# The last chunk of the input projection made by seven block products, with its weight sums and sigmoid around the SSM's group norms

## The reference

```
h = concat(meta_tokens, x)
u = rmsnorm(h, norm_mix_w)
proj = u @ w_in                     # hq hf hi hg | mq mk mv mo | z xbc | gates
y_a = hgrn2(...)      ; group_rmsnorm * silu(g)
y_b = mlstm(...)      ; group_rmsnorm(h, norm_w, 4 heads) * sigmoid(o_pre)
y_c = mamba2(...)     ; group_rmsnorm(y * silu(z), norm_w, 4 groups)
h = h + concat(y_a, y_b, y_c) @ w_out
h = h + moe(rmsnorm(h, norm_ffn_w)) # top group, top 2 experts of it, w1 w3 w2
out = rmsnorm(h, final_norm_w)[16:]
```

## Time and profile before

| | |
|---|---|
| time, median of 3 runs | 1479.79 us (1478.51 to 1480.06) |
| profiled execution, span | 1478.6 us |
| TensorE busy | 1273.7 us, 86% |
| weight loads of TensorE busy | 762.6 us, 52% |
| DVE / ACT / GpSimd busy | 536.3 / 280.4 / 211.7 us |
| moved by DMA | 487.76 MB, 330 GB/s in the mean |
| granted TensorE clock, mean | 0.916 of full |

### The profile page before, as it was taken

One profiled execution on the slowest core, in us unless ns is written; L12 is line 12 of the kernel. 1 busy time (PEld: TensorE's weight loads), 2 busy tenths in 40 slices (PEclk: granted clock), 3 DMA queues, 4 the chain that ended last, 5 costly groups with the idle time before them and its releaser, 6 DMA issues.

```text
span 1478.6 us, 20527 instructions
## 1 busy us (share of the span) xinstructions
PE 1273.7 (86%) x8658; PEld 762.6 (52%) x8658; DVE 536.3 (36%) x1204; ACT 280.4 (19%) x424; POOL 211.7 (14%) x158
## 2 busy tenths in 40 slices
PE   9999999999999999877876787688768867797797
PEld 7898899879999994222322232223223222232243
DVE  3554567434533215532332232223222321322235
ACT  3212414112150023111111111111111110110003
POOL 3180055015525720000000000000000000000000
PEclk9999999999999999988888888988888887798799
DMA  8653353445358649999999999999999999999997
GB/s 239 214 171 113 95 143 115 150 135 168 114 183 332 228 147 420 433 428 431 432 430 430 433 432 433 431 433 430 433 430 433 431 430 433 428 409 426 435 429 335
DMA packets 106769, 487.76 MB, mean 330 GB/s; under 512 B 19996, under 2 KB 91960, under 8 KB 92760
## 3 DMA queue, kind: packets, MB, share of 16 engines
q1 hardware_dynamic: 104176, 481.01, 80.8%
q0 software_dynamic: 1392, 5.47, 1.1%
q10 hardware_dynamic: 1130, 0.24, 0.1%
HBM read 482.36 MB, written 4.61 MB: 329 GB/s over the span
## 4 chain that ended last, share of the span: by engine, by line
PE 54%; DMA 43%; DVE 1%; issue 1%; POOL 1%; ACT 0%; SPq 0%; DVEq 0%; POOLq 0%
DMA big<-in_moe_w_dram 42%; PE bank L1748 22%; PE bank L2192 8%; PE bank L2107 5%; PE bank L2221 3%; PE bank L2234 3%; PE bank L1861 2%; PE bank L2161 2%; PE bank L2205 2%; PE bank L1898 1%; PE bank L1874 1%; DMA big<-in_w_in_dram 1%; PE bank L1940 1%; DMA big<-in_x_dram 1%; PE bank L2294 0%
## 5 line engine op out<-in xcount | busy, mean ns | idle before, releaser
L2192 PE MATMUL bank<-big 128*32 128x512 f32 x2016 | 295.0, 740 | 183.7 <-DMA big<-in_moe_w_dram 182.4
L1748 PE MATMUL bank<-big 128*128 128x128 f32 (+4 forms) x2288 | 361.2, 318 | 0.9 <-DVE colc L1170 0.5
L1748 PEld LDWEIGHTS bank<-big 128*128 128x128 f32 x2288 | 322.3, 191 | 30.6 <-issue 1.1
L2192 PEld LDWEIGHTS bank<-big 128*32 128x32 f32 x2016 | 74.6, 132 | 400.4 <-issue 211.1
L1581 DVE COPY big<-bank 128x512 f32<-128x512 f32 x32 | 22.1, 692 | 504.5 <-PE bank L2192 503.8
L1594 DVE TENSOR_TENSOR big<-big,bank 128x512 f32<-128x512 f32 x240 | 146.2, 681 | 12.3 <-PE bank L2234 12.3
L2221 PE MATMUL bank<-big 128*32 128x512 f32 x992 | 128.0, 662 | 0.5 <-DVE big L1586 0.5
L2234 PE MATMUL bank<-big 32*128 32x512 f32 x480 | 126.9, 633 | 0.7 <-ACT big L1029 0.7
L712 POOL COPY big<-big 32x512 f32<-32x512 f32 x4 | 2.4, 604 | 758.8 <-ACT big L1053 758.6
L1016 ACT ACTIVATE big<-bank 128x512 f32<-128x512 f32 x32 | 19.1, 597 | 355.1 <-PE bank L2161 355.1
L2221 PEld LDWEIGHTS bank<-big 128*32 128x32 f32 x992 | 31.8, 119 | 91.1 <-issue 90.1
(11 more groups left out here) (357 smaller groups left out, 1107.5 us busy)
## 6 DMA issues: line engine op xcount, KB each, us to landing
big<-in_moe_w_dram SPq DMA_DIRECT2D x92, 4096.0 KB, 32.6
big<-in_w_in_dram SPq DMA_DIRECT2D x25, 2048.0 KB, 8.3
big<-in_w_out_dram SPq DMA_DIRECT2D x7, 2048.0 KB, 8.2
big<-in_moe_w_dram SPq DMA_DIRECT2D x5, 2048.0 KB, 30.2
big<-in_moe_w_dram SPq DMA_DIRECT2D x6, 1024.0 KB, 6.9
h_rows<-big SPq DMA_DIRECT2D x1, 2176.0 KB, 13.8
big<-gate_rows POOLq DMA_DIRECT2D x8, 272.0 KB, 4.6
big<-h_rows SPq DMA_DIRECT2D x1, 2176.0 KB, 12.8
```

The lines of the kernel that those rows point to most:

```text
L1748: last = V.matmul(outs, a, b, start=start and j == 0, stop=stop and j == n - 1)
L2192: last = V.matmul(pb[2 + r][CAP * g:CAP * (g + 1), :], xsT[:, k % 4, k // 4, :], wk, start=j == 0, stop=j == 3)
```

## The change

`FOLD` gets chunk 25. With it:
- TensorE makes chunk 25 by seven block products, blocks 0 to 3 where its first half stood and 4 to 6 where the second half stood.
- GpSimd makes four more weight sums, behind the pair sum of the SSM's squares. They use the same places as before (in `xv`), so `rs4z` moves from `xv` to `mv`.
- ACT copies the first block product, and the sigmoid of the chunk is one instruction in place.
- The DVE makes the adds, three and two of them before the SSM's norm and two behind it.
- The first tiles of the output projection wait for those adds to have emptied their PSUM banks.
- Since `FOLD[-1]` is 25, SP reads `h` back behind chunk 27's load, and not behind chunk 26's.

```
--- before.py
+++ after.py
@@ -152,7 +152,7 @@
         PHs = PHb.rearrange("p (h c) -> p h c", h=4)
         mlo = PHb[:, 0:4 * T].rearrange("p (h t) -> p h t", h=4)
         mden = PHb[:, 4 * T:5 * T]
-        rs4z = xv[:, :, :].rearrange("p a c -> p (a c)")[:, 0:4 * T].rearrange("p (h t) -> p h t", h=4)
+        rs4z = mv[:, :, :].rearrange("p a c -> p (a c)")[:, 0:4 * T].rearrange("p (h t) -> p h t", h=4)
         Wb = scr(2 * 4 * T)
         W = [Wb[:, i * 4 * T:(i + 1) * 4 * T].rearrange("p (h t) -> p h t", h=4) for i in range(2)]
         sq8 = Wb.rearrange("p (h t) -> p h t", h=8)
@@ -225,7 +225,7 @@
         oh = part(13056, NA * CAP).rearrange("p (a s) -> p a s", a=NA)
         wo = part(13120, NA * P).rearrange("p (a c) -> p a c", a=NA)
         wT = part(13376, NA * P)
-        FOLD = (4, 5, 6, 11, 12, 13, 14, 19, 20, 21, 22, 23, 24)
+        FOLD = (4, 5, 6, 11, 12, 13, 14, 19, 20, 21, 22, 23, 24, 25)
         NF = len(FOLD)
         HT = T // 2
         START, cur = [], 0
@@ -667,10 +667,11 @@
             pool.wait_ge(s["e_ready"], SSH // 2)
             spread_rows(floor_rows, SSH + MLH, MLH).then_inc(s["floor_rows_in"], 16)
             for c in FOLD:
-                if 17 < c:
+                if 17 < c < 25:
                     weight_sums(c)
             pool.wait_ge(s["sq_ready"], 3)
             V.tensor_tensor(sq8[:, 0:4, NM:T], sq8[:, 0:4, NM:T], sq8[:, 4:8, NM:T], ALU.add).then_inc(s["pairs_added"], 1)
+            weight_sums(25)
 
 
             def fold1(c):
@@ -954,11 +955,12 @@
             squares(s["ssm_gated"], 1, proj[:, Z0:Z0 + 8, :].rearrange("p (g j) t -> p j g t", j=2),
                     sq8.rearrange("p (j g) t -> p j g t", j=2))
             inverse_rms(1, 1, rs4)
+            first_product(25)
             act.wait_ge(s["in_ev"], 4 + 50)
             V.activation(proj[:, MO:MO + 2, NM:T], proj[:, MO:MO + 2, NM:T], ACT.Sigmoid).then_inc(s["z_gate"], 1)
-            tile_out(50, ACT.Sigmoid)
             inverse_rms(2, 2, rs4z)
-            tile_out(51, ACT.Sigmoid)
+            act.wait_ge(s["in_ev"], 4 + 52)
+            V.activation(proj[:, MO + 2:MO + 4, NM:T], proj[:, MO + 2:MO + 4, NM:T], ACT.Sigmoid).then_inc(s["z_gate"], 1)
 
 
             def token_squares(a, rows, sums_to, junk):
@@ -1202,15 +1204,18 @@
                 dve.wait_ge(s["fold_added"], 4 * n + 2)
                 add(hi0, lo1, 3).then_inc(s["fold_added"], 1)
 
-            def adds_b(c):
+            def adds_b(c, parts=(0, 1)):
                 if c not in FOLD:
                     return
                 n = FOLD.index(c)
                 add, lo0, lo1, hi0, hi1 = block_adder(c)
-                dve.wait_ge(s["fold_ps"], 5 * n + 5)
-                dve.wait_ge(s["fold_added"], 4 * n + 3)
-                add(hi1, hi0, 4)
-                add(lo1, lo1, 4).then_inc(s["fold_added"], 1)
+                if 0 in parts:
+                    dve.wait_ge(s["fold_ps"], 5 * n + 5)
+                    dve.wait_ge(s["fold_added"], 4 * n + 3)
+                    add(hi1, hi0, 4)
+                    add(lo1, lo1, 4).then_inc(s["fold_added"], 1)
+                if 1 not in parts:
+                    return
                 dve.wait_ge(s["in_tile"], 2 * c + 1)
                 dve.wait_ge(s["in_ev"], 4 + 2 * c)
                 dve.wait_ge(s["fold_added"], 4 * n + 4)
@@ -1481,9 +1486,11 @@
             adds_a(24)
             adds_b(24)
             step.link(group_norm(1, mlo, rs4, 4, 1, PL))
+            adds_a(25)
+            adds_b(25, (0,))
             group_norm(2, proj[:, Z0:Z0 + 8, :], rs4z, 4, 2, PS).then_inc(s["z_done"], 1)
-            dve.wait_ge(s["z_gate"], 3)
-            dve.wait_ge(s["in_ev"], 4 + NIN)
+            adds_b(25, (1,))
+            dve.wait_ge(s["z_gate"], 4)
             for h in range(MLH):
                 last = V.tensor_tensor(proj[:, MO + h, :], proj[:, MO + h, :], mlo[:, h, :], ALU.mult)
             last.then_inc(s["norm_done"], 1)
@@ -2065,7 +2072,10 @@
                 c = u // 2
                 if u % 2 == 0:
                     pe.wait_ge((s["in_a"], s["in_b"])[c % 2], 16 * (c // 2 + 1) + (16 if u == NIN + NOUT - 2 else 0))
-                pe.wait_ge(s["in_ev"], u + 1)
+                if c - 1 in FOLD:
+                    pe.wait_ge(s["fold_added"], 4 * (NF - 1) + 3 + u % 2)
+                else:
+                    pe.wait_ge(s["in_ev"], u + 1)
 
             def by_rows(k):
                 pe.wait_ge(s["in_ev"], 4 + NIN + (k // 2 * 2 + 2 if k < NOUT - 2 else k + 1))
```

## The result

The changed kernel takes 1482.36 us (median of 11 runs, 1481.77 to 1482.73), the kernel before, on the same chip, 1478.58 (11 runs): ratio 1.0021, 95% interval 1.0013 to 1.0029. That is 3.8 us slower.

The account below looks back on a forecast made before the run. TensorE was taken to bound the kernel through the output projection, then expert-weight loads. Products -1.1 and chunk 28's lateness +2.3 gave +1.2 us on the median 1479.79: 1481.0 us, range for 8 in 10 1478.4 to 1483.6.

Parts of the forecast that it names:

- the likeliest case's own range: Whole kernel: the time range for the forecast case itself, 1480.0 to 1482.2 us; that case had chance 0.50.
- rival B: Output projection: slow queue, chunk 28 landing past 471.2, slower by more than 0.2%; price +4.0, 1483.8 us, chance 0.13.
- TensorE's own work: Chunk 25: folded products take 12.70 us instead of 13.81, gain 1.11 us, or 1.23 at the folded w_out rate.
- GpSimd, ACT, DVE at nothing: Around chunks 25 and 26: the added sums, copies, adds and shifted norms all come in time, cost nothing.
- The reload: SP's queue: h, now ahead of the first expert load and chunk 28, makes chunk 28 late, costing 2.3 us.
- the chunk is late by ... 2.3 us: Chunk 28: TensorE waits 1.7 us for its load and 0.6 us for GpSimd's third sum.
- The 0.6 for the third sum: Chunk 28: GpSimd's third sum, ending 7.2 us behind the landing, is wanted 6.6 us after TensorE's start.
- Bounds: Chunk 28's lateness: sum -0.4 at the best queue rate, -1.1 if all is hidden, +4.0 at the slow rate.
- Rival A: SP's queue: h's reload is free, so -1.1 us, 1478.7, or 1479.4 at the best rate; chance 0.27.
- the estimate from the Trainium skill: SP's queue: 2.0 us plus bytes at 436 GB/s has the four loads landed at 466.5, early enough.
- Rival C: Chunk 26: DVE's second norm ends past 443.6 and TensorE waits; say +1 on the forecast, 1482 us, chance 0.04.
- Within 0.2%: Whole kernel: time changes by under 3.0 us, chance 0.79, against 0.16 for slower and 0.05 for faster.

Follow-up runs that it names:

- e6: Changed kernel with the first expert load issued behind chunk 28's load and the second behind chunk 30's; 1478.08 us, 0.9994 of the kernel before.
- e1: Changed kernel with only the first expert load moved, issued behind chunk 28's load instead of ahead of it; 1479.14 us, 1.0001 of the kernel before.
- e4: Kernel before, chunk 25 plain, with the first expert load issued behind chunk 28's load; 1480.41 us, 1.0010 of the kernel before.
- e3: Changed kernel with five products, results never read, put before TensorE's wait for chunk 28; 1482.39 us, 1.0023 of the kernel before.
- e2: Kernel before, chunk 25 plain, with only h's reload moved behind chunk 27's load; 1483.83 us, 1.0030 of the kernel before.
- e7: Changed kernel with the first expert load cut, 2 MB ahead of chunk 28's load and 2 MB behind; 1478.12 us, 0.9993 of the kernel before.
- e10: Changed kernel with the wait for GpSimd's fourth sum moved from block 4 to block 6; 1482.87 us, 1.0025 of the kernel before.
- e9: e3 with the wait for GpSimd's fourth sum moved from block 4 to block 6; 1481.89 us, 1.0020 of the kernel before.

## Why the prediction was right, and where it was not

The range held the time and the place and cause of the loss were forecast; the forecast itself (+1.2 us) was a third of what was measured (+3.8, with +3.1 found in the trace), and the likeliest case's own range, up to 1482.2, was missed by 0.2. That the wide range held is in part luck. Its upper end came from rival B, a slow queue, and what filled the space was the clock, a term that the prediction did not have. And the sum was added to 1479.79, the median of three runs; the eleven runs beside the changed kernel gave 1478.58, and from there the range would have ended at 1482.4, where the measured time lies.

- **TensorE's own work**: forecast -1.1, the trace says -1.30, e6 -1.33 and e1 against e4 -1.27. I took chunk 24's 12.70 us; chunk 25 took 12.50. The other value that I named, 1.23, was nearer.
- **GpSimd, ACT, DVE at nothing**: right, each end within 0.4 us of its forecast, and no wait in the trace. The DVE's first norm took 3.41 us instead of 1.67 beside GpSimd's sum, which the prediction did not have; the slack covered it.
- **The reload**: right in place, cause and kind. I had chunk 28 landing at 469.4 (ends 468.8 and 470.0), it landed at 470.1: the expert load came 10.9 us behind h and not 9.9, chunk 28 then 5.7. Together with the earlier end of chunk 27 this made 2.7 us of idle time instead of 1.7, and 2.84 us of cost.
- **The step that failed**: "the chunk is late by ... 2.3 us, of which 1.7 is the load itself and 0.6 the sum". What was missing is what idle time does to TensorE: the granted clock was at 0.50 for 3.4 us, 3.1 of them on the blocks behind the wait, and these lost 1.57 us. I treated a wait as if it cost its own length. The 0.6 for the third sum was also too small. Its 7.2 us were counted from the start of the first sum, and not from the landing (456.82 - 449.45 = 7.4). And I took block 6 as the one that needs the fourth sum, but block 4 waits for it (e3: 0.78 + 0.71). In the changed kernel the slow clock hid both waits, so the terms are 2.84 and 1.57 in place of 1.7 and 0.6.
- **Bounds**: the trace's +3.1 lies inside -1.1 to +4.0. Rival A (the reload is free) is refuted by e2. With it falls the estimate from the Trainium skill (DMA: Bandwidth & Descriptors, Anatomy of one DMA), which had chunk 28 land at 466.5; the trace has 470.1. The page gives that fit for one DMA on GpSimd's path, and these were four loads on SP's queue, so it was the wrong fit to take. Rival B's price was nearly met, but not by its mechanism: the queue did not pass 471.2. Rival C did not come.
- **"Within 0.2%"** had 0.79; the measured ratio is 1.0021, just over, with an interval that reaches to both sides of the bound.
- The statement that a microsecond ahead of the experts is a microsecond at the end holds: the expert stretch lasted 911.2 to 912.1 us in all profiles but the one slow draw, with stretches ahead of it from 152.9 to 159.0.

What stays open is about 0.5 us: all the edited kernels are 0.3 to 0.8 us slower in the medians, against before, than their stretch says (e6: -1.33 in the stretch, -0.74 in the medians; changed: +3.11 and +3.8). It is the same with the fold and without it (e2, e4). No run tells whether it lies ahead of chunk 24 or in the experts: there the edited kernels' profiles (411.0 to 411.9 and 911.2 to 912.1 us) lie around those of the kernel before (411.2 and 911.8, without the slow draw).

e6 and e7 keep the fold and lose the wait. Their medians are 4.3 us under the changed kernel's, though not measured beside it, and 0.7 us under the kernel before, which their intervals (up to 1.0003 and 1.0002) do not tell from no change. What the fold can give here is 1.3 us in 1479.

## What to carry to other kernels

A buffer that a new step keeps in use longer moves whatever reloads it; follow that load to its new place in the queue and ask which transfer behind it has less slack than its bytes. Here it was the second one behind it, and giving way at one place made another one late (e1, e4), so look at the whole row of loads. Price a long wait of TensorE at more than its length (here 2.7 us of idle time cost 4.4 in all), and before removing a wait, look for the wait that it covers.

## What the runs showed of the hardware

- **Idle time of TensorE can cost more than its length.** With 2.7 to 2.9 us without work the granted clock went to 0.50 for 3.4 us (changed, e2, e10). It fell 0.3 us before the wait was over in the changed kernel, and 1.1 and 0.9 us after its end in e2 and e10; the blocks lost 1.57 us, and 1.73 in these two. With products in that time it stayed at 1.00 (e3, e9), and so it did around the shorter idle times of 0.4 to 0.5 us before blocks 3 and 4 in e3. The Trainium skill (TensorE: Matmul & The Clock Gate, The HAM clock gate) has the clock fall to 1.2 GHz when the array idles and rise when it has been busy. The traces agree, with the fall up to 1.1 us later than the idle time.
- **GpSimd and the DVE hold each other up.** The mLSTM's norm, four DVE instructions of 128x256 with both inputs in SBUF, took 3.41 us beside GpSimd's sum, and 1.67 in the kernel before, where GpSimd was idle. It is not that each takes twice as long. The first one alone took 2.22 us, until 430.78, just behind the end of the sum (428.14 to 430.50), and the other three 0.47 each; the first one in the kernel before took 0.48:

```profile
428.56 2.22 DVE L1368 SCALAR_TENSOR_TENSOR big<-big,par 128x256 f32<-128x256 f32 x1 [4.32 <-ACT big L881]
```

```profile
428.59 0.48 DVE L1363 SCALAR_TENSOR_TENSOR big<-big,par 128x256 f32<-128x256 f32 x1 [4.32 <-ACT big L880]
```

It was the same in e1, e6 and e10 (2.23 to 2.25 us). GpSimd's first sum for chunk 27 took 2.75 instead of 2.35 us where it began beside the DVE's last row sum (448.52, until 449.07). The Trainium skill (GPSIMD Engine Reference, Specifications) states such a contention for DVE instructions with two SBUF inputs. Here it cost the DVE 1.7 us once and GpSimd 0.4. I had costed the sums without it; there was slack for it here.
